# Expert weights of a mixture layer: two experts' halves side by side in HBM and loaded with one transfer

## What is computed

```python
def hier_moe(h, w_grp, b_grp, w_exp, b_exp, w_gate, w_up, w_down):
    # p_grp picks one of 4 groups a token; the top 2 of the group's 8 experts get gates
    ...
    return grouped_experts(hf, expert_idx, gates, w_gate, w_up, w_down).reshape(B, S, D)

# in grouped_experts, for every block of tokens of one expert e:
    hb = jax.nn.silu(xb @ w_gate[e]) * (xb @ w_up[e])
    return hb @ w_down[e]
```

## Time and profile before

| | us |
|---|---|
| median of 3 runs | 2842.57 (2830.61 to 2849.82) |
| the profiled execution | 2836.06 |
| its span, first to last instruction | 2834.2 |
| TensorE busy in the span | 2421.3 (85%) |
| VectorE, ScalarE, GpSimd busy | 1432.9, 704.3, 879.8 |
| moved by DMA | 694.84 MB in 109860 packets |

### The profile page before, as it was taken

The page is one execution under the profiler, slowest core; times in us unless marked ns, Lnnn a source line. Parts: engine busy times, 40 slices in busy tenths (PEclk is TensorE's granted clock), DMA queues, the critical chain, the costliest instruction groups (busy, mean ns, idle before and its releaser), DMA issues.

```text
span 2834.2 us, 40407 instructions
## 1 busy us (share of the span) xinstructions
PE 2421.3 (85%) x15976; PEld 1682.0 (59%) x15976; DVE 1432.9 (51%) x1927; ACT 704.3 (25%) x991; POOL 879.8 (31%) x520
## 2 busy tenths in 40 slices
PE   7998869987998889979885789989867868889885
PEld 6986649976997679934683433333356653334332
DVE  7876667876965478633764322212166561222213
ACT  3333423324333433312210111111123421111110
POOL 5888788888830068200242100000001000000000
PEclk9998879988999899989897999999988879999998
DMA  7765436765764156533102799999933129999995
GB/s 292 244 245 179 164 119 223 251 222 180 253 209 139 60 208 240 190 120 121 47 11 79 305 421 421 421 422 422 421 145 134 55 87 419 418 419 421 421 422 238
DMA packets 109860, 694.84 MB, mean 245 GB/s; under 512 B 14423, under 2 KB 15767, under 8 KB 34855
## 3 DMA queue, kind: packets, MB, share of 16 engines
q1 hardware_dynamic: 88704, 618.10, 55.9%
q0 software_dynamic: 21024, 74.99, 7.6%
q10 hardware_dynamic: 14, 0.06, 0.0%
HBM read 691.99 MB, written 1.11 MB: 245 GB/s over the span
## 4 chain that ended last, share of the span: by engine, by line
PE 48%; DMA 26%; DVE 9%; POOL 8%; issue 6%; ACT 2%; SPq 1%; POOLq 0%; DVEq 0%; ACTq 0%
PE bank L672 46%; DMA ring<-in_moe_wup 11%; DMA ring<-in_moe_wgate 11%; POOL wkx L2592 2%; DMA wkx<-in_ada_w 2%; PE bank L670 2%; POOL wkx L2596 2%; POOL wkx L2598 1%; DVE ring_r L1857 1%; POOL B L2592 1%; SPq L582 1%; POOL mix_t L2601 1%; POOL B L2604 0%; DMA B<-in_ada_w 0%; DMA const<-in_const 0%
## 5 line engine op out<-in xcount | busy, mean ns | idle before, releaser
L672 PE MATMUL bank<-ring,B 128*64 128x512 f32 (+1 forms) x3264 | 779.2, 597 | 114.7 <-DMA ring<-in_moe_wgate 69.0
L1857 DVE TENSOR_TENSOR ring_r<-ring,B_r 128x2048 fp32r<-128x2048 f32 x184 | 526.7, 2882 | 221.1 <-ACT B_r L1416 220.8
L672 PEld LDWEIGHTS bank<-ring,B 128*64 128x64 f32 (+1 forms) x3264 | 268.9, 140 | 582.5 <-issue 569.4
L672 PE MATMUL bank<-B_r 128*128 128x512 f32 (+1 forms) x1928 | 513.6, 353 | 17.6 <-DVE B L2100 9.7
L1416 ACT ACTIVATE B_r<-ring 128x2048 fp32r<-128x2048 f32 x184 | 347.0, 1908 | 318.2 <-PE bank L672 315.9
L672 PE MATMUL bank<-xt_r,B_r 128*128 128x256 f32 x1408 | 401.2, 285 | 24.5 <-issue 8.9
L672 PEld LDWEIGHTS bank<-B_r 128*128 128x128 f32 x1928 | 334.6, 194 | 111.1 <-issue 57.2
L672 PE MATMUL bank<-xt_r,ring_r 128*128 128x256 f32 x1408 | 399.2, 283 | 0.0
L672 PEld LDWEIGHTS bank<-xt_r,B_r 128*128 128x128 f32 x1408 | 269.1, 191 | 27.9 <-issue 24.5
L672 PEld LDWEIGHTS bank<-xt_r,ring_r 128*128 128x128 f32 x1408 | 270.5, 192 | 0.0
L670 PE MATMUL bank<-const,B 128*128 128x128 f32 x688 | 124.8, 345 | 144.6 <-issue 25.0
(11 more groups left out here) (334 smaller groups left out, 3052.2 us busy)
## 6 DMA issues: line engine op xcount, KB each, us to landing
ring<-in_moe_wgate SPq DMA_DIRECT2D x128, 1024.0 KB, 8.5
ring<-in_moe_wup SPq DMA_DIRECT2D x128, 1024.0 KB, 8.7
ring<-in_moe_wdown SPq DMA_DIRECT2D x128, 1024.0 KB, 9.9
ring<-in_ffn_w_gate SPq DMA_DIRECT2D x44, 1024.0 KB, 4.9
ring<-in_ffn_w_up SPq DMA_DIRECT2D x44, 1024.0 KB, 4.9
ring<-in_ffn_w_down SPq DMA_DIRECT2D x44, 1024.0 KB, 4.9
wkx<-in_ada_w POOLq DMA_DIRECT2D x72, 512.0 KB, 6.2
B<-in_ada_w POOLq DMA_DIRECT2D x24, 512.0 KB, 8.2
```

What stands on the lines that cost most here:

```text
L672: ins = pe.matmul(out, lhsT, rhs, start=start, stop=stop, skip_group_check=True)
L1857: dve.tensor_tensor(ring_r[:, slot, :], ring[:, slot, :], f32(hi), ALU.subtract).then_inc(sp_lo, 1)
```

## The change

On the host, the three expert arrays are laid out as [layer, pair, half, partition, expert of the pair, 2048]: the same half of both experts lies side by side, 16 KB a partition, and the 2 MB of a pair's half is one contiguous block. On the chip, `load_two` takes two neighbouring slots, waits until both are free, and issues one transfer of 2 MB into both (16 KB a partition); it signals `w_landed` of the even slot alone. PE's `two_units` waits once, for that semaphore. `Cursor` learns that in these loops the odd slots' semaphores don't rise. The matmuls, their order and the signals that free the slots are as before.

```diff
+    def take_two(self):
+
+        slot, landed, _ = self.take()
+        assert slot % 2 == 0
+        return slot, landed, self.take(0)[2]
...
     @contextmanager
-    def loop(self, eng, n, per):
+    def loop(self, eng, n, per, two=False):
 
         assert per % R == 0
+        self.lap = [16 * per // R * (not (two and x % 2)) for x in range(R)]
...
+            def load_two(src):
+
+                slot, _, pos = cur.take_two()
+                sp.wait_ge(w_free, pos)
+                sp.dma_start(ring[:, slot:slot + 2, :].rearrange("p s n -> p (s n)"), src).then_inc(w_landed[slot], 16)
+
...
             def moe(l):
-                g = A["moe_wgate_2"][l].rearrange("(i e) (p u k) n -> i e u p (k n)", e=2, u=2, p=P)
-                u = A["moe_wup_2"][l].rearrange("(i e) (p u k) n -> i e u p (k n)", e=2, u=2, p=P)
-                d = A["moe_wdown_2"][l].rearrange("(i e) (p u c) n -> i e u p (c n)", e=2, u=2, p=P)
-                with cur.loop(sp, PAIRS, 12) as i:
-                    for w in (g, u, d):
+                ws = [A[f"moe_w{x}_2"][l] for x in ("gate", "up", "down")]
+                with cur.loop(sp, PAIRS, 12, two=True) as i:
+                    for w in ws:
                         for half in range(2):
-                            for e in range(2):
-                                load((0, w[i, e, half]))
...
+                            load_two(w[i, half])
...
+            def two_units():
+                slot, landed, _ = cur.take_two()
+                pe.wait_ge(w_landed[slot], landed)
+                return slot, slot + 1
...
-                        s = [unit(), unit()]
+                        s = two_units()
...
-                    s = [unit(), unit()]
+                    s = two_units()
...
+    for x, rows in (("gate", D // 2 // P), ("up", D // 2 // P), ("down", D // 4 // P)):
+        w = arrays[f"moe_w{x}_2"]
+        w = w.reshape(LAYERS, PAIRS, 2, P, 2, rows * w.shape[-1]).transpose(0, 1, 4, 3, 2, 5)
+        arrays[f"moe_w{x}_2"] = np.ascontiguousarray(w.reshape(LAYERS, PAIRS, 2, P, 2 * UNIT))
```

More of the change, by code:

```diff
@@ L122, in take @@
             return slot, self.lots[slot], self.pos
-        return slot, self.i * (16 * self.per // R) + self.lots[slot], self.i * self.per + self.pos
+        return slot, self.i * self.lap[slot] + self.lots[slot], self.i * self.per + self.pos
+    def take_two(self):
+        slot, landed, _ = self.take()
+        assert slot % 2 == 0
+        return slot, landed, self.take(0)[2]
     def skip_second_trunk(self):
-        for dmas in [1] * 12 + [3, 1, 2, 1] + [1] * (4 + 12 * PAIRS):
+        for dmas in [1] * 12 + [3, 1, 2, 1] + [1] * 4 + [1, 0] * (6 * PAIRS):
             self.take(dmas)
     @contextmanager
-    def loop(self, eng, n, per):
+    def loop(self, eng, n, per, two=False):
         assert per % R == 0
+        self.lap = [16 * per // R * (not (two and x % 2)) for x in range(R)]
         with eng.Fori(0, n) as i:
@@ L138, in loop @@
         self.pos += (n - 1) * per
-        self.lots = [x + (n - 1) * 16 * (per // R) for x in self.lots]
+        self.lots = [x + (n - 1) * y for x, y in zip(self.lots, self.lap)]
 def f32(ap):
@@ L628, in moe @@
             def moe(l):
-                g = A["moe_wgate_2"][l].rearrange("(i e) (p u k) n -> i e u p (k n)", e=2, u=2, p=P)
-                u = A["moe_wup_2"][l].rearrange("(i e) (p u k) n -> i e u p (k n)", e=2, u=2, p=P)
-                d = A["moe_wdown_2"][l].rearrange("(i e) (p u c) n -> i e u p (c n)", e=2, u=2, p=P)
-                with cur.loop(sp, PAIRS, 12) as i:
-                    for w in (g, u, d):
+                ws = [A[f"moe_w{x}_2"][l] for x in ("gate", "up", "down")]
+                with cur.loop(sp, PAIRS, 12, two=True) as i:
+                    for w in ws:
                         for half in range(2):
-                            for e in range(2):
-                                load((0, w[i, e, half]))
-                w = [x.rearrange("i e u p q -> (i e) p u q") for x in (g, u, d)]
+                            load_two(w[i, half])
                 with overflowed(sp, l):
[L640 to L644, removed]
+                    with sp.Fori(0, PAIRS) as i:
+                        for e in range(2):
+                            sp.wait_ge(ov_step[l], i * 2 + (e + 1))
+                            for j in range(3):
+                                for half in range(2):
+                                    sp.dma_start(ring[:, 2 * j + half, :], ws[j][i, half, :, e * UNIT:(e + 1) * UNIT])\
+                                        .then_inc(ov_landed[l], 16)
                     sp.wait_ge(ov_step[l], N_EXP + 1)
@@ L1034, in moe @@
                 quad(n, first=True)
-                with cur.loop(pe, PAIRS // 4 - 1, 48) as i:
+                with cur.loop(pe, PAIRS // 4 - 1, 48, two=True) as i:
                     quad(n + 2, i)
```

## The result

| | before | after |
|---|---|---|
| median, us | 2837.85 (2829.97 to 2857.75, 20 runs) | 2868.16 (2847.13 to 2888.05, 20 runs) |
| profiled execution, us | 2836.06 | 2847.13 |
| its span, us | 2834.2 | 2845.4 |

The ratio after to before is 1.0094, with a 95% interval of 1.0069 to 1.0119: slower by nearly 1%, where a gain of 0.5% was forecast, and outside the range given. The profiled execution is the fastest of the 20; it is 11 us longer than the profiled one of before, where the medians differ by 30 us. (The ratio is not the quotient of the two medians, which can differ from it by some 0.2%.)

What follows compares the result with a forecast made beforehand. The prediction took the DMA engines' rate in both mixture layers as the bound. Saving 14.5 us and adding nothing took profiled 2836.1 to 2821.5, or 2828 us against the runs' median of 2842.57; range 2810 to 2846.

Steps and rivals of the forecast that it cites:

- What bounds the kernel: In both mixture layers the DMA engines, never stopping at 421 GB/s, set the pace; PE has some 3 us spare a pair.
- What the change removes: Mixture-layer loads: longer packets and half the completions save 78 ns per 2 MB, 186 transfers, 14.5 us; about 428 GB/s.
- (b): Rival, expert loads: descriptors are still cut at 8 KB, so only completions go, 1.6 us, 2841 us; chance 14%.
- (d): Rival, expert loads: 16 KB packets run slower, about 1.02 us each, costing 600 us, 3440 us; chance 4%.
- What it adds: Ring refills: waiting until both slots are free costs nothing, covered by 2 MB, 4.9 us, in flight.
- the two tight refills: Refills of down's half 1 and half 0: 9.6 and 9.5 us allowed, 7.4 needed, 2.2 and 2.1 to spare.
- the owed free: Second slot of down's half 1, freed only after a matmul of the next pair, at about 1814.54 + 0.3.
- the gain of 14.5 us: Both mixture layers: 186 transfers of 2 MB, each 78 ns shorter; about 7 us less a layer.
- rival (c): Behind down's half 1 the coarser refill lets DMA engines run dry, 32 us per microsecond late; 2860 at 1.0 late; chance 10%.
- The fixed 2 us: Per-transfer cost from the skill page; its formula would save 372 us, which the forecast set aside as covered by the queue.

Runs made afterwards that it cites:

- e3: Kernel before, 1 MB transfers, but both slots awaited ahead of the two issues; 2853.06 us, 1.0041.
- e10: Changed kernel with two unused matmuls a pair, before gate's half 1 and right behind down's half 1, the latter carrying the owed free; 2853.25 us, 1.0038.
- e5: Changed kernel with gate's half 1 and up's half 0 loaded as two 1 MB transfers each, slot by slot; 2851.52 us, 1.0007.
- e4: Changed kernel, but the refill of down's half 1 waits for ScalarE's signal that down is done; 2851.73 us, 1.0032.
- e8: Kernel of e3, but the refill of down's half 1 waits for ScalarE's early signal, as in e4; 2842.02 us, 0.9993.
- e9: Changed kernel with one added matmul a pair, its result unused, before the wait for gate's half 1; 2866.09 us, 1.0079.
- e11: Kernel of e5 with both added matmuls of e10; 2835.42 us, 0.9968 against the kernel before.
- e1: Kernel before with the new HBM layout alone, loads still 1 MB in 8 KB runs; 2840.78 us, 0.9989.
- e7: Changed kernel with only gate's half 1 split into 1 MB transfers, and e4's early signal for up's half 0; 2845.57 us, 1.0010.
- e2: Changed kernel's 2 MB transfers and waits on the old layout, so packets of 8 KB; 2863.6 us, 1.0066.

## Why the prediction was wrong

**What bounds the kernel: right.** The mixture layers follow the DMA rate. In e3, where only a wait was changed, the rate and the time moved together.

**What the change removes: right in mechanism and about in size, in the clear stretches.** 16 KB packets go uncut, so (b) is out, and (d) with it. The forecast had 610 ns a packet and 428 GB/s. DMA of after in 1799 to 1801, in the middle of a transfer:

```profile
q1 hardware_dynamic: 53, 0.87, 101.2%
```

53 packets in 32.38 us are 611 ns each. The middle of a pair runs at 426 to 429 GB/s, e10's layer 1 at 426, e5's at 425. That no version kept this gain over whole executions is a matter of the next step. The landing times of 10.3 to 10.7 us lie in the 9 to 11 given.

**"What it adds": the step that failed.** It was costed at nothing, because the 2 MB behind down's half 1 had 9.6 us to land and needed 7.4. This treats the 16 DMA engines as one queue that is dry only when its last transfer has landed. The runs show a price in its place: 19.4 us more in the two layers of the profiled execution where 14.5 less were forecast. Three things were wrong with the step.

First, the engines don't end together. DMA of after in 1801.4 to 1802 (first line) and in 1802 to 1804 (second line), its small packets being completions:

```profile
DMA packets 25, 0.25 MB, mean 410 GB/s; under 512 B 10, under 2 KB 10, under 8 KB 10
...
DMA packets 59, 0.87 MB, mean 434 GB/s; under 512 B 6, under 2 KB 6, under 8 KB 6
```

Of one transfer's 16 completions 10 fall into the first stretch and 6 into the next 2 us. The descriptors must be there when the first engine is through, 2 us and more before the transfer has landed for PE (the change at 1811.2 is 2.9 us ahead of gate's half 0 in PE at 1814.15). That used up the 2.1 and 2.2 us to spare of the two tight refills. Lateness against the landing was computed; the lead against the first engine had to be. For gate's half 1 it is not the wait for two slots that counts: before issues it at 1810.30, after at 1810.15. The place was on the edge already, and in before three packets there take 0.63 to 0.72 us in place of 0.31, at 1811.9 to 1812.5. Why after pays more at nearly the same issue time is not shown.

Second, the owed free was put at 1814.54 + 0.3. It came 1.1 us after the pair's start, 1815.23 against 1814.15. The trace of before had this already: its timeline of 1813 to 1817 gives the two issues behind down's half 1 by themselves,

```profile
1813.60 2.35 SPq L582 DMA_DIRECT2D ring<-in_moe_wup  x2
```

so the second went out at 1813.60 + 2.35 - 0.33 = 1815.62, 1.1 us after 1814.54. There it did no harm, since the first had gone out 2 us earlier.

Third, an issue can come before the first engine's end and still cost something: issues that come 1.05 and 1.4 us ahead of the first engine's end are followed by packets of 0.82 and 1.00 us in place of 0.61, much as the first packets on an idle queue, at 46.3 in before. The forecast had no such term. What a packet waits for in this time the trace doesn't tell.

The price follows from the same numbers. If the gain of 14.5 us is in the layers, and they are 19.4 us longer all the same, the stalls take 34 us, 1.06 a pair. The packets account for it: 632 ns in 1700 to 1900 against 610 is 22 ns for each of an engine's 48 packets a pair, 1.06 us. Most of it lies at the two changes, 1.01 us a pair in layer 1 and 0.68 in layer 2 (the sums given with e4). This is the place and the mechanism of rival (c), which was given 10%; its threshold ("from 2.7 us more than I assume") was wrong because the 2.2 us to spare in it did not exist. Its own test was wrong too: it asked for slices with 8 tenths of DMA share, and no slice of after has that. The share counts the slow packets in full; the GB/s beside it showed the fault.

The Trainium skill (Perfetto Trace Analysis, "DMA Optimizations") was quoted in the forecast on smaller chunks that may start sooner, and set aside because the rows showed busy engines. The runs side with its first half: split at both tight places, the transfers lose nothing that the times show (e5, 1.0007 [0.9974, 1.0040]), though the engines' share had been 0.99 and 1.00 in after, and not idle as the page supposes.

**Where the rest of the median's 30 us is.** The layers of the profiled execution, the fastest of 20, explain 19.4 us. The other 11 are not shown by an experiment. The table has one part of the answer: the rest of the span, which no edit touches, varies from 1869.2 to 1903.5 us, and some 20 us of that arise in the stage between the two layers alone. That stage in 2230 to 2250 (columns as above), first before, then e8, which has before's rate in the layers:

```profile
2230.00:2250.00 20.00, 20.00 (x182) 17.37 (x180) 14.79 (x66) 11.18 (x45) 0.00 (x0) 1.00 0.01 2
2230.00:2250.00 20.00, 20.00 (x99) 17.38 (x98) 6.35 (x33) 7.08 (x29) 0.00 (x0) 0.50 0.00 1
```

At the lower level of the clock (0.50, 1.2 GHz) PE gets 99 matmuls done in place of 182, and e8's stretch between the layers is 291.4 us long against 277.6. The profiled executions of e4, e5, e9 and e11 have the same (288.2 to 297.2 us), those of after and e10, the fastest of their kernels, have not (276.5 and 276.8). So executions differ by 12 us or more in a stage where all these kernels are alike, and where it is longer the clock is lower.

The list of runs fits this, and says no more than that time and clock go together. Over the 31 runs of the kernel before beside e1, a least-squares line gives 2.8 us more for each 0.001 of mean granted clock less; over the 25 beside e5 it gives 1.4. The 20 runs of after have a mean of 0.9278, those 31 of 0.9309, so some 9 of the 30 us go together with a lower clock by the first line and 4 by the second. e5's 10 runs have 0.9279 against 0.9308, which is 4 to 8 us of a difference of 7.8 in the medians; e11's have 0.9342, the highest of all, and that is as good a reason for its lead as its packets. Whether merged transfers make the lower clock outside the layers more frequent, or chance did in these runs, is open, and so is what makes executions of after spread over 41 us. Inside the layers e7's rows show a stall of PE, then 3.4 us at the lower level, then later frees; but e9 filled the idle time and won nothing clear, so which comes first is open there too. A ring of more slots would take all the refills off the edge; it was not tried.

## What to carry to other kernels

When transfers are merged, compute for each refill when the *last* of its slots goes free and when the *first* DMA engine ends the transfer ahead of it; that difference decides, not the time to the landing (here 1.05 and 1.4 us were too little, 2.5 us was enough). Look above all at the slot whose free is put off to a later instruction, and move that signal before you merge (here one ScalarE signal, or a spare matmul, gave back about half of the loss). A saving of a few ns a packet was worth nothing here until the next descriptors were always there in time, and GB/s in stretches of 5 us shows whether they are, not the busy share. And where executions of one kernel differ by 1%, time the changed stage itself in each profile: here its 19 us and the 8 of the rest had the opposite sign.

## What the runs showed of the hardware

- A run of 16 KB from HBM to SBUF moves in one packet, of 0.611 us in a full queue (1799 to 1801 in after); 8 KB takes 0.309.
- The first packets on an idle queue took 0.98 us for 8 KB (46.3 in before), and those behind an issue that came 1.4 us ahead of the first engine's end 1.00 us for 16 KB (1816.6 in after). Issues 1.05 and 1.4 us ahead were late, 2.5 us ahead was in time.
- The 16 engines end a transfer of 2 MB over some 2 us (10 completions in 0.6 us, 6 in the next 2), and the busy share stays near 1 while packets are slow: 1.01 at 374 GB/s.
- A 2 MB transfer has no worth of its own here. The Trainium skill (DMA: Bandwidth & Descriptors, "Rules for kernel authors") asks for 1 MB or more; the runs agree as far as that 1 MB in a queue already reaches 421 GB/s (e1), and going beyond it lost 0.7 to 0.9% (e2, after). The fixed 2 us that the forecast took from that page are given there for transfers that GpSimd issues; these are SyncE's, and no such time showed in the queue.
- Drops of the granted clock to 1.2 GHz appear in the mixture layers of some kernels with stalls (e7: 0.66 at 1815), where the profiles of before and of after have 1.00 over both long stretches. Between the layers one execution has 0.50 for 20 us where another has 1.00 (e8 and before, 2230 to 2250); the stage with the lower clock is 13.8 us longer.
